# Two causal convolutions that accumulate in a PSUM bank, three banks for the gate products, and a soft-plus series behind the convolution

## The reference

```python
def causal_dwconv(x, w):
    out = xp[:, 0:s] * w[0]
    for j in range(1, k):
        out = out + xp[:, j:j + s] * w[j]
...
# LRU: gates from the convolved half, then a first-order recurrence
xb = causal_dwconv(xb, conv_w) + conv_b
gates = sigmoid(einsum(xb by blocks of 128, gate_w) + gate_b)
log_a = -8.0 * r_t * softplus(-lam)
...
# delta net: q, k, v are convolved, z is not
qkv = silu(causal_dwconv(proj[..., :3072], conv_w))
g = -exp(a_log) * softplus(a_in + dt_bias)
o = chunk_gated_delta_rule(l2norm(q), l2norm(k), v, g, beta)
```

## Time and profile before

| | |
|---|---|
| median of three runs | 2746.71 us (2746.7 to 2747.99) |
| profiled execution, its own time | 2747.25 us |
| its span, first to last instruction | 2745.5 us |
| busy: TensorE, VectorE, ScalarE, GpSimd | 2500.6, 1884.3, 1072.5, 666.6 us |
| mean granted clock of TensorE | 0.943 of 2.4 GHz |
| LRU layer, chunk products | 2317.22 to about 2379 us |
| delta-net layer, chunk products | 2447.75 to 2561.88 us |

### The profile page before, as it was taken

How to read it: one execution, slowest core, us unless ns; L and a number is a source line. 1 busy time by engine, 2 the same in 40 slices (tenths; PEclk the granted TensorE clock), 3 DMA queues, 4 the chain that set the end, 5 groups by cost and what they waited for, 6 DMA issues and landing times. The chain is left out here.

```text
span 2745.5 us, 43327 instructions
## 1 busy us (share of the span) xinstructions
PE 2500.6 (91%) x15398; PEld 2238.2 (82%) x15400; DVE 1884.3 (69%) x3364; ACT 1072.5 (39%) x1798; POOL 666.6 (24%) x628
## 2 busy tenths in 40 slices
PE   7879878999999999888797899999999997687898
PEld 7747767999999999786576779999999996687897
DVE  7576997666666666596679976666666666659552
ACT  4321534444444444333224444444444444534321
POOL 4591473000000000066715800000000002436240
PEclk9869999999999999997798999999999998889898
DMA  5424303555555555444332055555555553234101
GB/s 202 143 97 160 116 1 107 190 187 189 184 185 189 186 188 183 154 154 138 133 129 83 1 165 187 184 187 188 188 186 184 188 187 122 94 127 138 52 1 39
DMA packets 107672, 392.39 MB, mean 143 GB/s; under 512 B 11952, under 2 KB 13360, under 8 KB 107184
## 3 DMA queue, kind: packets, MB, share of 16 engines
q1 hardware_dynamic: 107568, 391.02, 42.6%
HBM read 389.93 MB, written 1.05 MB: 142 GB/s over the span
## 5 line engine op out<-in xcount | busy, mean ns | idle before, releaser
L620 PE MATMUL bank<-chunk_parts,weight_parts 128*128 128x512 f32 x3072 | 748.1, 393 | 7.2 <-DVE chunk_parts L1235 7.2
L608 PEld LDWEIGHTS bank<-x_parts,chunk_parts 128*128 128x128 f32 x5760 | 722.5, 191 | 18.6
L1235 DVE TENSOR_TENSOR chunk_parts<-weight_ring,chunk_parts 128x1024 fp32r<-128x1024 f32 x496 | 605.9, 1222 | 178.8 <-ACT chunk_parts L840 178.8
L608 PE MATMUL bank<-x_parts,chunk_parts 128*128 128x256 f32 x5760 | 728.2, 283 | 0.0
L840 ACT CAST chunk_parts<-weight_ring 128x1024 fp32r<-128x1024 f32 x496 | 518.9, 1047 | 364.3 <-PE bank L620 364.3
L620 PEld LDWEIGHTS bank<-chunk_parts,weight_parts 128*128 128x128 f32 x3072 | 563.8, 189 | 118.7 <-DVE chunk_parts L1235 10.2
L1227 DVE TENSOR_TENSOR work<-work,big 128x256 f32<-128x256 f32 x256 | 162.8, 636 | 277.6 <-ACT work L844 261.3
L844 ACT ACTIVATE work<-bank 128x256 f32<-128x256 f32 x240 | 92.2, 384 | 440.3 <-PE bank L608 440.3
L884 POOL MEMSET big<- 128x572 f32 x2 | 1.1, 575 | 720.7 <-issue 714.6
L1528 PE MATMUL bank<-x_parts,chunk_parts 128*128 128x256 f32 x1152 | 150.3, 294 | 26.8 <-POOL chunk_parts L1518 26.8
L1434 POOL MEMSET big<- 128x24 f32 x1 | 0.1, 124 | 713.3 <-issue 713.3
(11 more groups left out here) (373 smaller groups left out, 3016.2 us busy)
## 6 DMA issues: line engine op xcount, KB each, us to landing
weight_ring<-in_experts SPq DMA_DIRECT2D x512, 512.0 KB, 3.3
big<-in_ada SPq DMA_DIRECT2D x48, 512.0 KB, 4.3
weight_ring<-in_w_in SPq DMA_DIRECT2D x40, 512.0 KB, 4.2
weight_ring<-in_wq SPq DMA_DIRECT2D x32, 512.0 KB, 3.5
weight_ring<-in_gdn_in SPq DMA_DIRECT2D x32, 512.0 KB, 3.4
weight_ring<-in_w_out SPq DMA_DIRECT2D x16, 640.0 KB, 4.0
weight_ring<-in_lru_in SPq DMA_DIRECT2D x16, 512.0 KB, 3.3
weight_ring<-in_w_kv SPq DMA_DIRECT2D x8, 512.0 KB, 4.6
```

What stands on the lines that cost most here:

```text
L608: last = nc.tensor.matmul(nc_ps[2 + n % 2][:, 0:T], a[:, j * P:(j + 1) * P], xr[:, x, j], start=(j == 0 and a is hi and x == 0), stop=(j = ...
L620: last = nc.tensor.matmul(nc_ps[4 + 2 * tt + c][:, 0:512], wr[:, x, n % 2, tt * P:(tt + 1) * P], v[:, c * 512:(c + 1) * 512], start=False, ...
L1235: nc.vector.tensor_tensor(split[:, k % SPLITS, 1], wring[:, (N_RING + k) % WSLOTS, 0:D], split[:, k % SPLITS, 0].bitcast(F32), ALU.subtrac ...
```

## The change

`causal_conv` gets a bank as one more argument, ps[7] in both layers. The first tap and the next two are written to it (half a bank for each tile of the pair), and the last tap reads it and writes the destination in SBUF. The gate products of the LRU layer use three banks (4 to 6) in place of four, and gate product i waits for sigmoid i - 3 in place of i - 4. `softplus` is cut in two: the first part as far as ScalarE's Exp, and `softplus_series`. The LRU layer calls the series, and the two scalings behind it, after the convolution; the delta-net layer calls both parts in a row, as before.

```diff
     link(nc.vector.tensor_tensor(w[0], w[0], z, ALU.min))
     dve.sem_inc(s("sp_in"), 1)
+
+
+def softplus_series(nc, dve, link, s, out, z, w):
+
     dve.wait_ge(s("sp_exp"), 1)
     link(nc.vector.tensor_scalar(w[1], w[0], 2.0, None, ALU.add))
...
-                    if i >= 4:
-                        pe.wait_ge(s("gates_kept"), i - 3)
-                    nc.tensor.matmul(ps[4 + i % 4][:, 0:T], wt[:, n], xc[:, n], start=True, stop=True).then_inc(s("gates"), 1)
+                    if i >= 3:
+                        pe.wait_ge(s("gates_kept"), i - 2)
+                    nc.tensor.matmul(ps[4 + i % 3][:, 0:T], wt[:, n], xc[:, n], start=True, stop=True).then_inc(s("gates"), 1)
...
-                    nc.scalar.activation((rt, it)[g][:, n], ps[4 + i % 4][:, 0:T], ACT.Sigmoid,
+                    nc.scalar.activation((rt, it)[g][:, n], ps[4 + i % 3][:, 0:T], ACT.Sigmoid,
...
             softplus(nc, dve, link, s, sp, small[:, 24:32], w4)
+            causal_conv(nc, dve, s, "kept", "convolved", LH, xpad, xc, par, Q_LCW, par[:, Q_LCB:Q_LCB + LH], ps[7])
+            softplus_series(nc, dve, link, s, sp, small[:, 24:32], w4)
             link(nc.vector.tensor_scalar(small[:, 16:24], sp, RG_C, None, ALU.mult))
             link(nc.vector.tensor_scalar(sp, sp, -RG_C, None, ALU.mult))
             dve.sem_inc(s("sp_ready"), 1)
-            causal_conv(nc, dve, s, "kept", "convolved", LH, xpad, xc, par, Q_LCW, par[:, Q_LCB:Q_LCB + LH])
...
-def causal_conv(nc, dve, s, ready, done, tiles, src, dst, par, at, bias):
+def causal_conv(nc, dve, s, ready, done, tiles, src, dst, par, at, bias, bank):
+
+    acc = bank[:, :].rearrange("p (a t) -> p a t", a=2)
...
-                    ins = nc.vector.tensor_scalar(dst[:, n], x, tap, 0.0 if bias is None else bias[:, n:n + 1], ALU.mult, ALU.add)
+                    ins = nc.vector.tensor_scalar(acc[:, n - n0], x, tap, 0.0 if bias is None else bias[:, n:n + 1], ALU.mult, ALU.add)
                 else:
                     dve.wait_ge(s(done + "_tap"), count - 2)
-                    ins = nc.vector.scalar_tensor_tensor(dst[:, n], x, tap, dst[:, n], ALU.mult, ALU.add)
+                    ins = nc.vector.scalar_tensor_tensor(dst[:, n] if j == CTAPS - 1 else acc[:, n - n0], x, tap, acc[:, n - n0], ALU.mult, ALU.add)
...
             softplus(nc, dve, link, s, gg, ab, w4)
+            softplus_series(nc, dve, link, s, gg, ab, w4)
...
-            causal_conv(nc, dve, s, "kept", "convolved", 3 * LH, pad, qkv, par, Q_GCW, None)
+            causal_conv(nc, dve, s, "kept", "convolved", 3 * LH, pad, qkv, par, Q_GCW, None, ps[7])
```

## The result

| | before | after |
|---|---|---|
| median | 2747.35 us (4 runs, 2746.7 to 2750.29) | 2729.74 us (4 runs, 2728.84 to 2730.41) |
| span of the profiled execution | 2745.5 us | 2727.8 us |
| second block: from GpSimd's first memset of the LRU layer to the end | 446.4 us | 427.0 us |

The ratio is 0.9937, 95% interval [0.9922, 0.9952]; 17.6 us by the medians, 2728.8 us forecast. It is the better measure: in the profiled executions of this study the first block, which no kernel here changes, ends anywhere from 2293.7 to 2303.8 us, while the second block agrees within 0.3 us between kernels that should have the same one (before and e2; change, e1 and e6; e7 and e10). Each kernel has one profiled execution, so its scatter within a kernel isn't shown otherwise.

The account below looks back on a forecast made before the run. VectorE's convolution, waiting for GpSimd, was taken to hold TensorE in the delta-net layer: 14.6 waits + 2.7 clock + 7 x 0.2 refilling - 0.8 Square = 17.9 us off, 2746.7 - 17.9 = 2728.8 us, own range 2727 to 2731.

Parts of the forecast that it names:

- What bounds: Delta-net layer: VectorE's convolution, waiting for GpSimd, sets the pace at 7.4 us a pair against TensorE's 5.76.
- Release: Convolution instructions with one SBUF input and the bank as other input or output no longer wait for GpSimd.
- L1497 still waits: Rival: the first tap still waits for GpSimd; one wait costs nothing, two give 2746 to 2749 us; 0.05 with no release.
- no release at all: Rival: L1500 waits for GpSimd in either form, 2746 to 2748 us; chance 0.05 together with two waits.
- the slower one: Rival: VectorE's traffic on bank 7 holds TensorE's writes to banks 0 to 3, 2755 us at half pace; chance 0.03.
- Own cost: A convolution pair without waits takes 3.5 us, bounds 3.2 and 6.4 us.
- surcharge of 65 ns for a PSUM source: Skill page's price for each instruction reading a bank: 0.5 us more a convolution pair, still hidden.
- Limit of 5.8 us: Delta-net convolution: a pair costing up to 5.8 us is free, hidden behind TensorE's chunks.
- Square: Delta-net layer: ScalarE's Square of 3.63 us still leaves TensorE a stall of 0.8 us, without clock loss.
- Sum: Copies of chunks 5 to 31 in the delta-net layer: 17.9 us come off.
- Everything behind chunk 31 shifts: All work behind chunk 31 in the delta-net layer follows TensorE and moves earlier with it.
- LRU layer: No gain: TensorE waits for the second gate weight until 2354.99; series taking 25 us, covered; three banks cost 0.

Follow-up runs that it names:

- e2: Kernel before with only the three LRU-layer edits; the delta-net convolution still accumulates in SBUF: 2748.79 us, ratio 1.0008.
- e1: Changed kernel with the bank accumulator in the delta-net layer alone, LRU layer as before: 2732.04 us, ratio 0.9949.
- e6: Changed kernel with the last tap of the delta-net convolution issued three times, four more instructions a pair: 2728.67 us, ratio 0.9938.
- e7: Changed kernel with the two gate weights loaded early into idle SBUF instead of through the ring: 2716.05 us, ratio 0.9887.
- e10: e7 with the soft-plus series in front of the LRU convolution again: 2723.08 us, ratio 0.9911.
- e3: Changed kernel with the last tap of the delta-net convolution issued five times, eight more instructions a pair: 2736.17 us, ratio 0.9961.
- e5: Changed kernel with only the first tap written to the bank, the later taps written to SBUF: 2737.84 us, ratio 0.9976.
- e4: Changed kernel with the first tap also written to SBUF by an extra instruction a tile: 2727.26 us, ratio 0.9926.
- e8: Kernel before the change, with the two gate weights loaded early: 2744.66 us, ratio 0.9995.
- e9: Changed kernel with ScalarE's Square over 16 tiles cut in eight, each behind its SiLU: 2731.48 us, ratio 0.9936.
- e11: Changed kernel with early gate weights and the Square in parts together: 2722.09 us, ratio 0.9908.

## Why the prediction was right

**What bounds.** Right: VectorE's waits for GpSimd set the pace of the delta-net layer through ScalarE (e3, e5 and e6 show the limit from both sides), and removing them gave the pace back to TensorE.

**Release.** Right for L1500's successor, and for L1497's, where only L1930's 156 ns spoke for it; e4 shows that the same instruction with both ends in SBUF does wait. The rivals "L1497 still waits" and "no release at all" are out. So is the slower one: chunks are 2.88 us apart beside VectorE's work in bank 7, in e6 too, where a pair takes 4.9 us of it.

**Own cost.** 3.5 us a pair forecast, 3.36 measured. The surcharge of 65 ns for a PSUM source that the prediction worked out from the Trainium skill (VectorE: DVE Perf Modes, The TRN2 errata) isn't seen: 481 ns with input and output in the bank, 475 with the input alone, 478 before. (Six instructions a pair read the bank, so by that price it would have been 0.4 us a pair and not 0.5.)

**Limit of 5.8 us.** Bracketed: 5.0 costs nothing (e6), 6.2 and 6.5 cost 10 and 13 us of the second block (e5, e3). What I had not counted is that such stalls run together behind the Square and pull the clock down, so beyond the limit the loss is larger than 12 pairs' excess.

**Square.** 0.8 us of stall forecast, 0.74 measured.

**Sum.** The stretch from chunk 5 to 31: 76.1 forecast, 76.27 measured; 17.9 against 17.7 us. "Everything behind chunk 31 shifts" was not quite right: the small products there were 1.6 us shorter (15.4 to 13.8, at a clock of 0.75 instead of 0.67) and the rest 0.4, while 0.2 was lost ahead of chunk 5. The second block as a whole fell by 446.4 - 427.0 = 19.4. In the profiled pair the first block was 1.7 us longer after the change, which makes 17.7 of it; the agreement with 17.9 is in part that accident.

**LRU layer.** Right: nothing (e2), and for the reason given: the gate weights (e7, e8). The series took 9.5 us, not 25, and ended at 2357.50, since only two of its instructions met GpSimd, which was idle from 2353.60 on; its move and the three banks cost and give nothing (e1, e10).

## What to carry to other kernels

When VectorE and GpSimd run side by side and an elementwise chain on VectorE shows two lengths, its own and its own plus one GpSimd instruction, put the intermediate into a free PSUM bank; but first work out by when each piece is wanted, since freeing it beyond that is worth nothing, as here in the LRU layer. Before polishing an engine's work, give the next releaser in line its cure as well: the early gate weights made the same convolution worth 8 us more and are the fastest version here (2716.05 us). And compare stretches from a landmark inside the execution, since a gain of 2 us is lost in the scatter of a part that nobody changed.

## What was not expected of the hardware

- Less waiting made later work slower. From the copy of chunk 31 to TensorE's next instruction behind the 96 small products it took 13.77, 15.40 or 17.03 us, with granted clocks of 0.75, 0.67 and 0.60, and nothing between. In all three the clock falls to 0.50 while TensorE is busy with these products and comes back before their end; by the mean clocks that stretch is about 6.9, 10.2 and 13.6 us long. 15.40 belongs to the kernels whose TensorE had fallen to half clock behind a long stall in the chunks (before, e2, e3, e4, e5, e8), 13.77 to those with only the 0.74 us stall (change, e1, e6, e7, e10), 17.03 to the two without any (e9, e11). What decides it was not tried.
- An instruction of VectorE with one SBUF input waits for GpSimd when its output is in SBUF (e4, up to 2555 ns), and not when its output is in a bank (max 548 ns).
